# Attention's opening in a hybrid decoder layer: sample softmax, sample values and the recurrence's reload set at other steps

## The reference

```
x += 0.5 * SwiGLU_1(RMSNorm(x))
P  = RMSNorm(x) @ W_in        # RWKV-7 columns, attention q/k/v, two branch gates
A  = RWKV7(P_rw)              # delta-rule recurrence, 8 heads of 64
B  = DiffAttn(q, k, v)        # 4 heads, softmax map 1 minus lambda * softmax map 2
x += (sigmoid(Ga) * (A @ W_pa) + sigmoid(Gb) * (B @ W_pb)) @ W_out
x += 0.5 * SwiGLU_2(RMSNorm(x));  y = RMSNorm(x)
```

## Time and profile before

| what | value |
| --- | --- |
| profiled execution | 2706.64 us, span on the core 2705.0 us |
| PE busy | 2594.2 us, 96% of the span |
| DVE / ACT / POOL busy | 1713.4 / 804.1 / 591.7 us |
| mean granted clock of PE | 0.977 of full speed |
| last projection unit evicted | 1275.2 us from the span's start |
| first scores | 1282.3 us |
| last attention product ends | about 1481 us |

### The profile page before, as it was taken

The page is one execution under the profiler, slowest core; times in us unless marked ns, Lnnn a source line. Parts: engine busy times, 40 slices in busy tenths (PEclk is TensorE's granted clock), DMA queues, the critical chain, the costliest instruction groups (busy, mean ns, idle before and its releaser), DMA issues.

```text
span 2705.0 us, 55099 instructions
## 1 busy us (share of the span) xinstructions
PE 2594.2 (96%) x22506; PEld 2459.8 (91%) x22506; DVE 1713.4 (63%) x2086; ACT 804.1 (30%) x1321; POOL 591.7 (22%) x534
## 2 busy tenths in 40 slices
PE   7999999999999999998788999979999999999998
PEld 7999999999999999998345899869999999999998
DVE  5877777422484688677776777675587777763223
ACT  6333333101211222332444222221343333331012
POOL 2333332000010232111101645220023333320000
PEclk9999999999999999999798999979999999999999
DMA  5233332751323545667965001043323333236411
GB/s 196 85 105 98 120 98 62 274 180 57 109 93 99 157 153 170 210 203 261 318 208 165 26 25 31 19 146 110 125 75 111 106 99 112 73 106 202 154 47 71
DMA packets 293398, 342.12 MB, mean 126 GB/s; under 512 B 22324, under 2 KB 217744, under 8 KB 293024
## 3 DMA queue, kind: packets, MB, share of 16 engines
q1 hardware_dynamic: 252960, 189.42, 23.5%
q0 software_dynamic: 40000, 149.17, 15.3%
q10 hardware_dynamic: 192, 0.07, 0.0%
HBM read 254.32 MB, written 84.28 MB: 125 GB/s over the span
## 4 chain that ended last, share of the span: by engine, by line
PE 86%; DVE 9%; issue 1%; DMA 1%; ACT 1%; DVEq 0%; SPq 0%; POOL 0%; ACTq 0%
PE ps L2359 42%; PE ps L2487 31%; PE ps L2721 1%; DVE small L1987 1%; PE ps L2741 1%; PE ps L2736 1%; PE ps L2404 1%; DMA q_rot<-q_save 1%; DVE probs L2009 1%; PE ps L2579 1%; PE ps L2768 1%; PE ps L2748 1%; PE ps L2622 1%; DVE kq_prod L1854 1%; PE ps L2776 1%
## 5 line engine op out<-in xcount | busy, mean ns | idle before, releaser
L2359 PE MATMUL ps<-h,w_hi 128*128 128x344 f32 x2112 | 506.4, 323 | 0.0
L2359 PEld LDWEIGHTS ps<-h,w_hi 128*128 128x128 f32 x2112 | 361.9, 188 | 17.4 <-issue 16.7
L2359 PE MATMUL ps<-h,w_lo 128*128 128x344 f32 x1056 | 336.7, 319 | 0.0
L1747 DVE SCALAR_TENSOR_TENSOR x_res<-ps,x_res 128x1032 f32<-128x1032 f32 x48 | 59.2, 1233 | 322.0 <-PE ps L2359 322.0
L2487 PE MATMUL ps<-t,w_hi 128*128 128x258 f32 x1408 | 259.2, 285 | 0.0
L1166 ACT ACTIVATE w_hi<-w_stage 128x512 fp32r<-128x512 f32 x252 | 157.7, 628 | 316.7 <-PE ps L2487 278.7
L2487 PE MATMUL ps<-t_one,w_hi 128*128 128x258 f32 x1280 | 234.3, 284 | 3.1 <-issue 2.6
L2487 PEld LDWEIGHTS ps<-t,w_hi 128*128 128x128 f32 x1408 | 219.8, 191 | 0.0
L1689 DVE TENSOR_TENSOR tmp<-tmp,ps 128x516 f32<-128x516 f32 x210 | 145.4, 692 | 106.6 <-PE ps L2487 94.1
L1658 DVE TENSOR_TENSOR w_lo<-w_stage,w_hi 128x512 fp32r<-128x512 f32 x252 | 193.0, 766 | 23.5 <-ACT w_hi L1166 0.9
L2487 PEld LDWEIGHTS ps<-t_one,w_hi 128*128 128x128 f32 x1280 | 198.9, 190 | 3.5 <-issue 3.5
(11 more groups left out here) (543 smaller groups left out, 6161.0 us busy)
## 6 DMA issues: line engine op xcount, KB each, us to landing
w_stage<-in_ffn_up SPq DMA_DIRECT2D x176, 256.0 KB, 3.0
key_ring<-in_cache_k SPq DMA_DIRECT2D x128, 256.0 KB, 3.0
value_ring<-in_cache_v SPq DMA_DIRECT2D x88, 256.0 KB, 3.0
w_stage<-in_w_in SPq DMA_DIRECT2D x84, 256.0 KB, 3.3
w_stage<-in_ffn_down SPq DMA_DIRECT2D x80, 256.0 KB, 3.3
g_save<-g_ring POOLq DMA_DIRECT2D x32, 516.0 KB, 4.8
g_save<-g_kept POOLq DMA_DIRECT2D x32, 516.0 KB, 4.8
x_res<-x_save POOLq DMA_DIRECT2D x6, 2064.0 KB, 9.0
```

Source lines behind the costliest of these rows:

```text
L1747: in_turn(v.scalar_tensor_tensor(ch3(xm), dense[s], 0.5, ch3(xm), ALU.mult, ALU.add) .then_inc(ev[f"psum_free{s}"], 1))
L2359: last = mm(dense[s][:, j], w[w0][:, k0 + k, :], column(r, k, slice(j * CH, (j + 1) * CH)), start=(k == 0 and n == 0), stop=(k == nk - 1 a ...
```

## The change

It has five parts. Groups of key pages: the last unit holds none, unit 27 two. The maximum over pages and POOL's maximum over partitions stand in unit 29, ahead of its eviction on DVE and ahead of its gate store on POOL. The sample softmax: piece 0 ahead of all maxima, the exponentials ahead of the first `probs`, piece 1 ahead of step 0, `sample_sums` in step 0, piece 2 in step 0. `FILL_STEP` starts at step 2, with two groups in steps 19, 22, 25 and 28. POOL's reload of the 20 operand transfers waits for `w_trans_lo` 6, the transposes of step 5. In addition PE waits for the second PSUM half only ahead of `scores(1)`.

```diff
-GROUPS_OF = [0 if n == 0 else 2 if n in (15, 20, 26) else 1 for n in range(UNITS)]
+GROUPS_OF = [0 if n in (0, UNITS - 1) else 2 if n in (15, 20, 26, 27) else 1 for n in range(UNITS)]
...
-        FILL_STEP = [s for s in range(HP, STEPS - 2) for _ in range(2 if s in (17, 19, 22, 25, 26, 28) else 1)]
+        FILL_STEP = [f + 2 for f in range(2 * HP * 2)] + [18 + 3 * b + k for b in range(NS // 2) for k in (0, 1, 1, 2)]
... POOL
+                if n == UNITS - 1:
+                    pool.wait_ge(*ev.at("s_max_part", 1))
+                    nc.gpsimd.partition_all_reduce(smax, smaxp, P, bass.bass_isa.ReduceOp.max).then_inc(ev["s_max_all"], 1)
                 if n >= ZT:
                     pool.wait_ge(*ev.at(f"gate_made{s}", p - ZPAIRS + 1))
...
-            pool.wait_ge(*ev.at("s_max_part", 1))
-            nc.gpsimd.partition_all_reduce(smax, smaxp, P, bass.bass_isa.ReduceOp.max).then_inc(ev["s_max_all"], 1)
             pool.dma_start(masks, A["const_table"][:, CONST_AT[LOOP_CONSTS]:NCONST]).then_inc(ev["masks_loaded"], 16)
...
             pool.wait_ge(*ev.at("z_rows_stored", 32))
+            pool.wait_ge(*ev.at("w_trans_lo", 6))
             for dst, src, done in ((KKn, kk_save, "kk_back"), (Bf, b_save, "b_back"), (Kf, kp_save, "kp_back"),
... ACT
+            sample_exp()
             probs(0)
...
-                if step == 0:
-                    sample_exp()
... DVE
+            smx = smaxp.rearrange("p (b m) -> p b m", b=NS)
...
+                if n == UNITS - 1:
+                    in_turn(v.tensor_reduce(smx, SC.rearrange("p (b g m) -> p b m g", b=NS, g=PAGES), AX, ALU.max)
+                            .then_inc(ev["s_max_part"], 1))
                 dve.wait_ge(*ev.at(f"unit_done{s}", c + 1))
...
+            sample_softmax(0)
             maxima(0)
             maxima(1)
+            sample_softmax(1)
...
-                if step < 3:
-                    sample_softmax(step)
+                if step == 0:
+                    sample_softmax(2)
... PE
-            pe.wait_ge(*ev.at("psum_free1", AT_MERGE))
...
             scores(0)
+            pe.wait_ge(*ev.at("psum_free1", AT_MERGE))
             scores(1)
...
-                if step == 2:
+                if step == 0:
                     sample_sums()
```

More of the change, by code:

```diff
@@ L1932, in _ @@
                         unit_keys(h)
-            smx = smaxp.rearrange("p (b m) -> p b m", b=NS)
-            in_turn(v.tensor_reduce(smx, SC.rearrange("p (b g m) -> p b m g", b=NS, g=PAGES), AX, ALU.max)\
-                .then_inc(ev["s_max_part"], 1))
             def pages(a):
```

## The result

The changed kernel took 2727.49 us (median, 2723.06 to 2731.64), the kernel before 2709.3 us (2707.47 to 2711.06). The ratio is 1.0069 with a 95% interval of 1.0054 to 1.0083: slower by 18.7 us (14.6 to 22.5) as the ratio has it; the medians differ by 18.2. The forecast was 2727. The profiled execution took 2723.06 us, its span is 2721.4 against 2705.0.

The account below looks back on a forecast made before the run. Bound in the changed stretch: a transfer, then DVE, then PE and DVE with DMA close behind. Terms 0 + 0.6 − 1.0 + 16 + 2 = +17.6 gave 2727 us from the median; range for 8 in 10, 2709 to 2736.

Parts of the forecast that it names:

- The reload: Steps 7 to 11: value groups land 8.1 us apart beside the late reload, so step 11 has its group +16 later.
- the upper bound of +20: Top of the reload term, +18 to +20, from 4.8 groups in 38.8 us with no group in hand.
- The lower bound of 0: Bottom of the reload term, if the value pages kept the 4.1 us a group that they need.
- the gate store's window: Profile rows in which q1 held 77% of the DMA engines against one gate store, a short transfer from SBUF.
- Queries and first scores: Opening: the queries' issue does not move, and the first scores come at 1282 ± 1; cost 0.
- Sample softmax: DVE's opening: piece 0 moves under PE's wait for the queries, at 1277 to 1279, gain 1.85 us.
- Values from step 2 on: Steps 2 to 15: two groups more eat the 1.85; step 5's transposes at 1313.5 against 1312.9, +0.6.
- Clock and doubled steps: PE at the lower clock when pages flow again, +2 (0 to +5); doubled step 26 becomes single, −1.0.
- Rival A: Steps 6 to 11: pages keep 240 GB/s beside POOL's queue, so 6.4 us faster, 2704; chance 0.15.
- Rival B: No change: starved steps lose only what steps 16 and up leave free, or under 5 us; 2706 to 2715; chance 0.17.
- Rival C: Scores start later, mask constants at about 1278 share engines with the queries, at most 1.1 us; 2728; within the forecast's 0.68.

Follow-up runs that it names:

- the wait alone: The kernel before with one edit, POOL's 20 reload transfers wait for the transposes of step 5: 2725.98 us against 2708.52, ratio 1.006.
- the best version: The changed kernel with FILL_STEP of before and the reload split, 10 transfers early and 10 one a step behind steps 16 to 25: 2705.19 us, ratio 0.9985.
- its two variants: The kernel before with the reload behind step 5's transposes, 2725.98 us, and with 10 transfers early, 10 one a step from step 16, 2705.62 us.
- the kernel before with the split reload: The kernel before with one edit, 10 reload transfers at the old place, 10 one a step behind steps 16 to 25: 2705.62 us against 2709.62.
- the last run: The best version with POOL's maximum over partitions placed behind the gate store of unit 29: 2710.84 us, ratio 1.0006 against the kernel before.

## Why the prediction was right, point by point

- **The reload** was the term that decided, and its mechanism is shown. The rate held (8.1 us a group forecast, 7.9 to 8.2 measured), packets went one for one, and the wait alone costs +16.3 in the kernel before. The term was +16 at step 11; measured +18.6. Group 5 came at 1327.8 instead of 1323: I had counted group 4 as about landed when the reload began, while its last pages were issued until 1314.0 and those of group 5 from 1314.81 on, so part of group 4 and all of group 5 shared the engines with the reload. The rule of the Trainium skill (DMA: Bandwidth & Descriptors, "Queues, rings and completion order"), round robin by packet, agrees with 583 to 584 and 882 to 885 packets.
- **Where the range stood:** the upper bound of +20 for this term holds. The lower bound of 0 rested on the gate store's window. There POOL's queue had 143 packets in all against SP's 691, so it could not share one for one for long; with 20 transfers in the queue SP's share is 36%.
- **Queries and first scores:** forecast 1282 ± 1, measured 1283.01, at its edge. The profiled execution of the changed kernel evicts unit 27 at 1257.07 instead of 1254.40, a shift of 2.7 us. 2.5 us of it are there by 51 us, where both kernels do the same work; PE's wait for the queries takes most of it up (6.41 us instead of 8.33).
- **Sample softmax:** this step failed in detail. Piece 0 was to run at 1277 to 1279, 1.85 us for nothing, with POOL's maximum 2.3 us behind DVE's. POOL's maximum ended at 1282.78, over 5 us behind DVE's (1277.41), and the gate store behind it was issued at 1282.66 instead of 1276.69, not under 1 us later. Piece 0 ran from 1282.82 to 1284.66, so it stood in front of the first maxima, and step 3's weights came at 1304.5 as before, not 1.3 earlier. A gain that I had anyhow counted as eaten by value work was eaten here.
- **Values from step 2 on:** forecast 1313.5 for step 5's transposes, measured 1312.50 (before 1312.87). PE works without a gap from 1303 and its clock comes back at about 1307, where a group still took 1.75 us at 1310.56 before; that this paid for the two groups more fits these rows and was not tested by itself.
- **Clock and doubled steps:** forecast +2 and −1.0 behind step 11. From step 11's group to the recurrence it took 142.8 us before (1338.95 to 1481.72) and 141.2 after (1357.57 to 1498.79): −1.6 together, forecast +1.0. The +2 for the clock was too high: in the kernel before with the late reload, which keeps the doubled steps, the same stretch took 141.6 us (1355.01 to 1496.58), −1.2 against before. For the same reason the −1.6 can't be put down to the single steps. The lower clock was granted in windows in which pages were awaited (0.67 from 1330 to 1340), where it hides behind the wait; from 1360 to 1370 the granted clock was 1.00. It fell to 0.83 once more from 1370 to 1380, as it did from 1350 to 1360 in the kernel before.
- **Sum:** up to step 11 +16.6 forecast and +18.6 measured, behind it +1.0 and −1.6: two errors of the size of 2 us cancelled, and that is luck. In all +17.6 forecast, +16.4 in the spans, +18.7 between runs. That 2727 was hit to half a us is luck as well: runs of the changed kernel lie between 2723 and 2732. (2710.04 + 17.6 is 2727.6; the prediction has it as 2727.)
- **Rival A** (faster, the reload covered) fell with the page rate. It named what the early start could gain; the best version shows −4.1 in place of the −6.4 worked out, by giving the reload another place. **Rival B** fell with the waits of 15.2 us. **Rival C** fell with the times: the mask constants went out at 1283.42, behind the first scores (1283.01), and not at 1278.

## What to carry to other kernels

A transfer that nobody awaits is not free. Queued in bulk on another queue, it here took the DMA engines packet for packet from the transfer that an engine did await, and as its packets were twice as large, two thirds of the engines' time. So look for the stretch in which no awaited stream runs (here DVE's opening), or hand it out one piece a step; the same 10.6 MB cost 16 us in bulk in the kernel before, and handed out one transfer a step in the changed kernel they cost nothing that could be measured. And price a moved operation by the queue that it lands in front of or behind, not only by its own duration.

## What the runs showed of the hardware that was not expected

POOL's maximum over partitions has a cost that its row (0.54 us) does not show. Behind the gate store it comes 6.59 to 7.40 us after the end of that store's issue in four kernels (before, its two variants, and the version with the maximum put back behind the store), even where its input was ready 3.4 us ahead of that. The POOL timeline of the kernel before with the split reload:

```profile
1279.00 0.53 POOL L915 DMA_DIRECT2D gate_save<-tmp  x1 [10.73 <-ACT tmp L1370]
1286.17 0.54 POOL L937 PARTITION_ALL_REDUCE rstd<-rstd  x1 [6.64 <-issue]
```

Placed ahead of the store, it comes 4.4 to 5.9 us after its input in eight kernels (the expectation of the last run has this as 4.8 to 5.8), and 9.2 to 10.8 us after POOL's last instruction. In the kernel before, part of the 6.6 us lay beside DVE's last key group, which made it look like 1.8 us. The Trainium skill (GPSIMD Engine Reference, "Instruction dispatch") gives about 6 us for loading code at the first call of a freshly loaded kernel; the 6.6 us behind the store are near it, but no run here took that load apart. Why the maximum takes 6.6 us from the store in one order and 4.4 to 5.9 us from its input in the other stays open.
